# A hybrid attention and gated-recurrence encoder block: five small reorderings around its queues

## Chip, cores and metric

One core of one Trainium2 chip. The metric is the device time of one execution, in microseconds (us), as a median over several runs.

## The reference

One layer over 1024 tokens of width 1024, all in float32:

```python
u = rmsnorm(h); proj = u @ w_in                      # 1024 x 4096
qa, ka, va, hq, hff, hfb, hi, hg = split(proj, 8)    # 512 columns each
y_na = neighbourhood_attention(qa, ka, va, ...)      # 8 heads of 64
k, log_f = gate(hff or hfb, lower_bound)             # f = lb + (1-lb)*sigmoid
# S_t = diag(f_t) S_{t-1} + k_t v_t^T ; o_t = S_t^T q_t   forward and backward
y_hg = rmsnorm(o_fwd + o_bwd) * silu(hg)             # 4 heads of 128
h = h + concat(y_na, y_hg) @ w_out
u = rmsnorm(h)
h = h + square(relu(u @ w_up)) @ w_down              # hidden 4096
```

## The kernel before

Every large product is made of three float32r products (high part times high part, high times low, low times high), so each operand is split into a high part (a rounded copy) and a low part (the difference). TensorE (PE) has a list of work written out by hand, and so have VectorE (DVE), ScalarE (ACT), GpSimd (POOL) and SyncE (SP, which issues most transfers). The engines meet by counting semaphores; each executes its own list strictly in order.

**Input weights.** The 32 column tiles of w_in (128 columns each) and the 8 row tiles of w_out are loaded by SP in turn into two slots of `stage`, and POOL splits them into a ring of four slots (`w_hi`, `w_lo`): tile n is split in two instructions, `w_hi` (stage times one) and `w_lo` (stage minus w_hi). The split of tile n waits until PE has used n-3 tiles (`w_used`); SP's load of tile n waits until tile n-2 is split (`w_split`, L727). Tiles 16 to 27 hold the recurrence's gates and queries (ff, fb, hq of heads 0 to 3), 28 to 31 the output gates hg, 32 to 39 w_out. Tiles 16 to 35 are split in a loop with a register (L864 to L867, the instructions at L845 and L848), 36 to 39 at L884 to L895. Ahead of the load of tile 36 SP also waits for the first level of head 3 and then loads the attention's results back (`na_back`, 2 MB, L721), and ahead of tile 37 it waits for the outputs of head 3 and loads the residual (L726).

**The recurrence.** Head by head (h = 0 to 3), each in ten pieces. Pieces 0 to 7 each have a level: PE multiplies keys by queries for two groups of four chunks (L2073), DVE multiplies the keys (`move_keys`, L1551 and L1554) and then, for each group, the queries (L1562) and copies the level's scores under a mask (L1567, `take_level`), which lets the level after the next start. Piece 8 has the chunk updates (transposes L2092, products L2100, on DVE the chain of states L1587), piece 9 the head's outputs (L2112 to L2116). Between them PE works off the projections of the next head in steps (`take_steps`; a step is 3 matmuls of 512 columns). A projection ends in a unit of ACT or DVE that empties its bank: for hq it is ACT's copy into `h_q` (L982), which level 0 of the next head waits for, and DVE's `first_queries` (L1530) too. ACT executes the units of a piece at the piece after it (`last`); in piece 9 it squares both halves of the head's outputs (`head_squares`, L1108) ahead of that. For heads 1 and 2 the second half of hq ends in piece 9 of the head before; for head 3 it ends in piece 8.

**The output projection.** Blocks of two row tiles: block 0 needs tiles 32 and 33 split, and `mixer_hi(0)` (L1130, ACT) and `mixer_lo(0)` (L1610, DVE) of na_back. `mixer_hi(0)` stands in piece 9 of head 3, ahead of the squares.

**The MLP.** Both products are made by a scheme of seven products of half-size blocks, which needs sums of blocks of operands. Of the tokens, T1 = high - low and T3 = high's right half - T1 are formed by POOL for each of four token tiles (`token_sums`, L906 and L908) once DVE has normalised the tile t+4 (L1382); T2 is then formed by DVE (`t2_sums`, L1745). PE transposes the sets (`turn_set`, L1952); the set of T1 and T3 waits for all eight sums (`t13_sum`). ACT takes each transposed set (L1139) and DVE its low part (L1391). The up projection's product waits for the low parts of its set (L2241), POOL forms the low parts of the weights (`up_lo`, L899). At the end DVE adds the results into `acc` (L1881), in quarters: the sums number 3 fill acc_a's right half, number 4 acc_b's right half, number 5 acc_a's left half, number 6 acc_b's left half, and SP stores acc_a and acc_b by whole token tiles of 512 KB after sums 5 and 6 (L828).

Of the kernel before, what the change touches and what calls it, by code (L numbers as in the profile page):

```python
# [10 lines left out]
ALU = mybir.AluOpType  # L11
# [3 lines left out]
D = 1024  # L15
S = 1024
KT = D // P
TT = S // P
HALF = 512
# [20 lines left out]
HG_HEADS = 4  # L40
# [30 lines left out]
DOWNS = 4  # L71
# [109 lines left out]
def hybrid_block(nc, x, w_in, w_out, attn_norm_w, mlp_norm_w, q_norm_w, k_norm_w, rpb, hg_norm_w,  # L181
                 lb_fwd, lb_bwd, w_up, w_down, tables, masks, out):
    ctx = ExitStack()
    with ctx:
# [451 lines left out]
        def _(sp):  # L636
# [185 lines left out]
                load_acts(m)  # L822

            out_v = out.rearrange("b (t p) d -> (b t) p d", p=P)
            for i in range(2):
                for t in range(4):
                    sp.wait_ge(summed, 28 * (DOWNS - 1) + 4 * (5 + i) + t + 1)
                    sp.dma_start(out_v[4 * i + t], acc[i][:, t, :]).then_inc(out_store, 16)  # L828
            sp.wait_ge(h_store, 16 * TT)
            for i in range(7):  # L830
                sp.wait_ge(a_store[i], 16 * UPS)
            sp.wait_ge(out_store, 16 * TT)

            sp.wait_ge(v_stored[0], 32 * 4)
            sp.wait_ge(v_stored[1], 32 * 4)
# [3 lines left out]
        def _(pool):  # L839
# [22 lines left out]
            def split_turns(first, end):  # L862

                with pool.Fori(first, end, 1) as r:  # L864
                    for i in range(RING):
                        split(i, r * (16 * RING // STAGE) + 16 * (i // STAGE + 1) - 32,
                              r * RING + (i + 1 - RING), r * (2 * RING) + 2 * i)  # L867
# [11 lines left out]
            for n in range(RING, 4 * RING):  # L879
                if 10 <= n < 16:  # L880
                    pool.wait_ge(bias_done, bias_ops(2 * n - 19))
                split_one(n)
            split_turns(4, N_TILES // RING - 1)
            for n in range(N_TILES - 4, N_TILES):  # L884
                pool.wait_ge(w_load[n % STAGE], 16 * (n // STAGE - 1))
                if n < N_TILES - 2:
# [24 lines left out]
                up_lo(n)  # L911
            for t in range(3):
                token_sums(t)
            token_sums(3)
            up_lo(4)
            up_lo(5)
            for n in range(6, 7 * UPS):
# [8 lines left out]
        def _(act):  # L926
# [176 lines left out]
            def head_squares(h):  # L1103
                for part in range(2):
                    act.wait_ge(o_done, 2 * h + part + 1)
                    if h:
                        act.wait_ge(o_norm, 2 * h)
                    act.activation(tmp[:, part, :], bank[6 + part][:, :], ACT.Square).then_inc(o_sq, 1)  # L1108
# [162 lines left out]
            for h in range(HG_HEADS):  # L1271
                for i in range(PIECES):
                    if 1 <= i <= NHALF:
                        copy_keys(h, i - 1)
                    if i == 0:
                        for n in last:
                            unit(n)
                        last = []
                        take_diagonal(h)
                        if h:  # L1280
                            head_roots(h - 1)
                    if i == 8:
                        take_k_tok(h)
                    for n in last:
                        unit(n)
                    if i == 9:
                        if h == HG_HEADS - 1:
                            mixer_hi(0)
                        head_squares(h)
                    last = HEAD_UNITS[h][i]  # L1290

            for n in last:
                unit(n)
# [73 lines left out]
        def _(dve):  # L1367
# [386 lines left out]
            for n in range(4, 8):  # L1754
                up_sum(n)
            normalise_tokens(1, TT - 1)
            for t in range(3):
                t2_sums(t)
            take_set(8)
# [124 lines left out]
        def _(pe):  # L1884
# [285 lines left out]
            for h in range(HG_HEADS):  # L2170
                for i in range(PIECES):
                    steps = UNIT_STEPS[h][i]
                    if i < NLEV:
                        level(h, i)
                        if i == 0 and h:
                            head_means(h - 1)
                        take_steps(steps)
                    elif i == 8:
                        chunk_products(h, lambda q: take_steps(steps[len(steps) * q // 4:len(steps) * (q + 1) // 4]))
                    else:  # L2180
                        take_steps(steps)
                        head_outputs(h)
# [124 lines left out]
```

## Time and profile before

| | |
|---|---|
| median of 3 runs (lowest, highest) | 1332.29 us (1330.5, 1332.58) |
| the profiled execution | 1328.1 us |
| its span | 1326.1 us |
| PE busy in the span | 1288.4 us (97%) |
| DVE, ACT, POOL busy | 868.7 us (66%), 583.4 us (44%), 481.4 us (36%) |
| granted TensorE clock | 0.999 of full speed |
| share of the chain that ended last | PE 85%, DVE 7%, ACT 3%, issue 3%, POOL 1%, DMA 1% |

An instruction of PE is shown as busy until its last result is out, and matmuls overlap: one of 512 columns lasts 0.39 us in the rows, but starts 0.23 us after the one before. "issue" is time in which the engine waited for nothing that the profile shows. The stages of the span by the lines of PE: values and tokens first, attention's products from 103 to 304 us, the recurrence behind them, the output projection from 599 to 693 us, the up projection to 1015 us, then the down projection.

### The profile page before, as it was taken

The page shows a single profiled execution, that of the slowest core. Times are in us where ns is not written, and L with a number is a line of the kernel's source. Part 1 is how long each engine was busy: PE and PEld are TensorE (multiplying, and loading weights), DVE is VectorE, ACT ScalarE, POOL GpSimd, SP SyncE. Part 2 cuts the span into 40 slices and gives each one's busy share as a digit, 9 for nine tenths or more (in the row PEclk, how much of TensorE's full clock was granted, in tenths as well). Part 3 has the DMA queues.
Part 4 walks back from the last instruction along what each step waited for, and adds up shares of the span by engine and source line. Part 5 has one row for each costly group of instructions (what it writes and reads, how often), then busy time and mean ns, then how long its engine had stood idle before and what let it go on. Part 6 is the DMA issues. An engine that isn't in the chain of part 4 may idle for free.

```text
span 1326.1 us, 17670 instructions
## 1 busy us (share of the span) xinstructions
PE 1288.4 (97%) x6432; PEld 1077.5 (81%) x6432; DVE 868.7 (66%) x1258; ACT 583.4 (44%) x1049; POOL 481.4 (36%) x261
## 2 busy tenths in 40 slices
PE   7999899999999999899999999999999999999998
PEld 5867787998888888787887788888888788888887
DVE  3456567541878686977457655455455898888885
ACT  5436566445335353333145545445544333432341
POOL 3251121125312132212424554545443454444452
PEclk9999999999999999999999999999999999999999
DMA  8341332322111011023420654444468563443433
GB/s 256 109 129 30 77 105 83 84 73 64 35 31 33 17 32 33 20 93 144 142 94 2 207 175 135 148 155 151 135 220 320 200 239 108 139 162 112 146 99 137
DMA packets 133172, 154.91 MB, mean 117 GB/s; under 512 B 11232, under 2 KB 89312, under 8 KB 133088
## 3 DMA queue, kind: packets, MB, share of 16 engines
q1 hardware_dynamic: 128880, 147.04, 34.5%
q10 hardware_dynamic: 4208, 6.76, 1.5%
q8 instruction: 53, 0.87, 0.3%
q14 instruction: 31, 0.25, 0.1%
HBM read 109.72 MB, written 44.04 MB: 116 GB/s over the span
## 4 chain that ended last, share of the span: by engine, by line
PE 85%; DVE 7%; ACT 3%; issue 3%; POOL 1%; DMA 1%; SPq 0%; ACTq 0%; DVEq 0%
PE bank L2272 8%; PE bank L2276 8%; PE bank L2275 8%; PE bank L2241 7%; PE bank L2244 7%; PE bank L2245 7%; PE bank L1989 5%; PE bank L1993 5%; PE bank L1992 5%; PE bank L2073 4%; PE bank L2198 2%; PE bank L2202 2%; PE bank L2201 2%; PE bank L1887 1%; PE bank L1979 1%
## 5 line engine op out<-in xcount | busy, mean ns | idle before, releaser
L922 POOL TENSOR_TENSOR a_split<-a_raw,a_split 128x1024 fp32r<-128x1024 f32 x56 | 148.1, 2662 | 166.0 <-ACT a_split L1195 166.0
L2241 PE MATMUL bank<-set,w_hi 128*128 128x512 f32 x448 | 177.8, 397 | 1.0 <-issue 0.6
L2244 PE MATMUL bank<-set,w_hi 128*128 128x512 f32 x448 | 176.2, 393 | 0.0
L2245 PE MATMUL bank<-set,w_lo 128*128 128x512 f32 x448 | 176.0, 393 | 0.0
L2272 PE MATMUL bank<-w_hi,a_split 128*128 128x512 f32 x448 | 174.7, 390 | 0.2
L2275 PE MATMUL bank<-w_lo,a_split 128*128 128x512 f32 x448 | 174.3, 389 | 0.0
L2276 PE MATMUL bank<-w_hi,a_split 128*128 128x512 f32 x448 | 174.3, 389 | 0.0
L1989 PE MATMUL bank<-uT_hi,w_hi 128*128 128x512 f32 x384 | 160.8, 419 | 2.6 <-DVE h_gate L1437 2.4
L1993 PE MATMUL bank<-uT_hi,w_lo 128*128 128x512 f32 x384 | 150.6, 392 | 0.0
L1992 PE MATMUL bank<-uT_lo,w_hi 128*128 128x512 f32 x384 | 150.0, 391 | 0.0
L845 POOL TENSOR_TENSOR w_hi<-stage,one_col 128x1024 fp32r<-128x1024 f32 x20 | 39.7, 1986 | 270.9 <-PE bank L1989 223.6
L899 POOL TENSOR_TENSOR w_lo<-stage,w_hi 128x512 fp32r<-128x512 f32 x56 | 75.2, 1347 | 86.6 <-ACT w_hi L1149 86.6
L899 POOL TENSOR_TENSOR w_lo<-raw_b,w_hi 128x512 fp32r<-128x512 f32 x56 | 74.5, 1336 | 73.5 <-ACT w_hi L1149 73.5
L2241 PEld LDWEIGHTS bank<-set,w_hi 128*128 128x128 f32 x448 | 84.2, 188 | 20.9 <-issue 1.3
L2245 PEld LDWEIGHTS bank<-set,w_lo 128*128 128x128 f32 x448 | 84.1, 188 | 19.2
L2272 PEld LDWEIGHTS bank<-w_hi,a_split 128*128 128x128 f32 x448 | 84.1, 188 | 18.8 <-issue 1.7
L2244 PEld LDWEIGHTS bank<-set,w_hi 128*128 128x128 f32 x448 | 84.2, 188 | 18.2
L2276 PEld LDWEIGHTS bank<-w_hi,a_split 128*128 128x128 f32 x448 | 84.1, 188 | 17.6
L2275 PEld LDWEIGHTS bank<-w_lo,a_split 128*128 128x128 f32 x448 | 84.1, 188 | 17.5
L1837 DVE TENSOR_TENSOR w_lo<-raw,w_hi 128x1024 fp32r<-128x1024 f32 x35 | 73.4, 2103 | 26.0 <-ACT w_hi L1186 26.0
L1989 PEld LDWEIGHTS bank<-uT_hi,w_hi 128*128 128x128 f32 x384 | 72.6, 189 | 17.7 <-DVE h_gate L1437 3.2
L1186 ACT ACTIVATE w_hi<-raw 128x1024 fp32r<-128x1024 f32 x35 | 36.9, 1054 | 110.7 <-DVE raw L1835 31.6
(223 smaller groups left out, 2805.7 us busy)
## 6 DMA issues: line engine op xcount, KB each, us to landing
a_raw<-a_dram SPq DMA_DIRECT2D x56, 512.0 KB, 3.6
a_dram<-abuf SPq DMA_DIRECT2D x111, 256.0 KB, 2.1
stage<-in_w_in SPq DMA_DIRECT2D x29, 512.0 KB, 4.3
raw<-in_w_down SPq DMA_DIRECT2D x10, 1024.0 KB, 8.3
stage<-in_w_up SPq DMA_DIRECT2D x16, 512.0 KB, 5.5
raw_b<-in_w_up SPq DMA_DIRECT2D x16, 512.0 KB, 5.6
x_tok<-in_x SPq DMA_DIRECT2D x8, 512.0 KB, 10.1
v_dram<-vs ACTq DMA_DIRECT2D x16, 256.0 KB, 2.4
```

Source lines behind the costliest of these rows:

```text
L899: pool.tensor_tensor(ring_part(w_lo, n), up_operand(*UP_SEQ[n]), ring_part(w_hi, n).bitcast(F32), ALU.subtract).then_inc(x_lo, 1)
L922: pool.tensor_tensor(split_of(m, 1), a_raw[:, m % 4, :, :], split_of(m, 0).bitcast(F32), ALU.subtract).then_inc(b_lo, 1)
L1837: dve.tensor_tensor(down_slot(w_lo, m), here, down_slot(w_hi, m).bitcast(F32), ALU.subtract).then_inc(v_lo_done, 1)
L1989: first = pe.matmul(b[:, :], w[0], u[0], start=k == 0, stop=False)
L1992: pe.matmul(b[:, :], w[0], u[1], start=False, stop=False)
L1993: ins = pe.matmul(b[:, :], w[1], u[0], start=False, stop=k == KT - 1)
L2241: first = pe.matmul(dst, w[0], u[0], start=k == 0 and p in (1, 5, 6, 7), stop=False, skip_group_check=True)
L2244: pe.matmul(dst, w[0], u[1], start=False, stop=False, skip_group_check=True)
L2245: ins = pe.matmul(dst, w[1], u[0], start=False, stop=k == 3, skip_group_check=True)
L2272: first = pe.matmul(dst, a[0], w[0], start=start, stop=False, skip_group_check=True)
L2275: pe.matmul(dst, a[0], w[1], start=False, stop=False, skip_group_check=True)
L2276: ins = pe.matmul(dst, a[1], w[0], start=False, stop=q == 1 and k == 1, skip_group_check=True)
```

## The change

1. In piece 9 ACT executes the hq units of that piece ahead of the squares, not after them.
2. PE takes two steps (6 matmuls) of piece 0 of head 0 ahead of level 0, not after it.
3. POOL's splits of tiles 32 to 35 are written out, and the one of tile 33 waits until all levels of head 3 are taken (`lev_taken` at 56). Tiles 34 and 35 stand behind it.
4. T1 and T3 of the last token tile are formed by DVE behind its last normalisation, ahead of the T2 sums, and POOL waits for them in their place ahead of `up_lo(4)`.
5. The output is stored by half token tiles of 256 KB, 16 stores in place of 8, each after the sum that completes it.

```diff
-            for i in range(2):
+            for i, half, s in ((0, 1, 3), (1, 1, 4), (0, 0, 5), (1, 0, 6)):
+                cols = slice(HALF * half, HALF * half + HALF)
                 for t in range(4):
-                    sp.wait_ge(summed, 28 * (DOWNS - 1) + 4 * (5 + i) + t + 1)
-                    sp.dma_start(out_v[4 * i + t], acc[i][:, t, :]).then_inc(out_store, 16)
+                    sp.wait_ge(summed, 28 * (DOWNS - 1) + 4 * s + t + 1)
+                    sp.dma_start(out_v[4 * i + t][:, cols], acc[i][:, t, cols]).then_inc(out_store, 16)
...
-            sp.wait_ge(out_store, 16 * TT)
+            sp.wait_ge(out_store, 16 * 2 * TT)
...
-            split_turns(4, N_TILES // RING - 1)
+            split_turns(4, N_IN // RING)
+            for n in range(N_IN, N_IN + RING):
+                if n == N_IN + 1:
+                    pool.wait_ge(lev_taken, HEAD_PARTS * HG_HEADS)
+                split_one(n)
...
-            token_sums(3)
+            pool.wait_ge(t13_sum, 8)
...
                     if i == 9:
                         if h == HG_HEADS - 1:
                             mixer_hi(0)
+                        early = [n for n in HEAD_UNITS[h][i] if UNITS[n][0] == "hq"]
+                        for n in early:
+                            unit(n)
                         head_squares(h)
-                    last = HEAD_UNITS[h][i]
+                    last = [n for n in HEAD_UNITS[h][i] if i < 9 or UNITS[n][0] != "hq"]
...
             normalise_tokens(1, TT - 1)
+            dve.wait_ge(u_ready, 2 * TT)
+            dve.wait_ge(t13_sum, 6)
+            low, high = u_tok[:, 3, 0:HALF], u_tok[:, TT - 1, 0:HALF]
+            dve.tensor_tensor(low, high, low, ALU.subtract).then_inc(t13_sum, 1)
+            dve.wait_ge(t13_sum, 7)
+            dve.tensor_tensor(high, u_tok[:, TT - 1, HALF:D], high, ALU.subtract).then_inc(t13_sum, 1)
             for t in range(3):
                 t2_sums(t)
...
                     if i < NLEV:
+                        ahead = 2 if (h, i) == (0, 0) else 0
+                        take_steps(steps[:ahead])
                         level(h, i)
                         if i == 0 and h:
                             head_means(h - 1)
-                        take_steps(steps)
+                        take_steps(steps[ahead:])
```

## Rows read from the trace of the kernel before

**Rows 1.** Waits of PE over the whole span (total us, times, longest us).

```profile
PE bank L2073 <- issue: 3.2, 3, 1.2
```

**Rows 2.** Timeline, PE and ACT at the turn from head 0 to head 1.

```profile
399.14 2.02 PE L2073 MATMUL bank<-h_q,k_both 128*128 128x128 f32 x16 [1.22 <-issue]
...
398.45 0.59 ACT L982 ACTIVATE h_q<-bank 128x512 f32<-128x512 f32 x1
```

**Rows 3.** Timeline of PE, DVE and POOL at the start of head 0.

```profile
338.41 2.02 PE L2073 MATMUL bank<-h_q,k_both 128*128 128x128 f32 x16 [0.73 <-issue]
...
349.24 2.42 PE L2073 MATMUL bank<-queries,near_keys 128*128 128x128 f32 x16
...
338.35 2.36 DVE L1530 TENSOR_TENSOR queries<-forget,h_q 128x1024 f32<-128x1024 f32 x2 [5.61 <-ACT h_q L982]
...
341.76 2.84 DVE L1551 TENSOR_TENSOR near_keys<-near_keys,forget 128x512 f32<-128x512 f32 x1
344.52 3.33 DVE L1554 TENSOR_TENSOR far_keys<-near_keys,forget 128x512 f32<-128x512 f32 x1
...
348.37 0.72 DVE L1567 COPY_PREDICATED scores<-hg_mask,bank 128x512 f32<-128x512 uint8 x1
...
340.75 2.84 POOL L845 TENSOR_TENSOR w_hi<-stage,one_col 128x1024 fp32r<-128x1024 f32 x1 [9.27 <-PE bank L1989]
```

**Rows 4.** Timeline of PE, DVE and POOL in the levels of head 3.

```profile
560.67 1.13 PE L2073 MATMUL bank<-queries,near_keys 128*128 128x128 f32 x8 [0.83 <-DVE scores L1567]
563.42 1.13 PE L2073 MATMUL bank<-queries,near_keys 128*128 128x128 f32 x8 [1.62 <-DVE scores L1567]
568.37 0.50 PE L1989 MATMUL bank<-uT_hi,w_hi 128*128 128x512 f32 x1 [1.07 <-DVE h_gate L1437]
...
557.50 2.38 DVE L1562 TENSOR_TENSOR queries<-queries,decay 128x512 f32<-128x512 f32 x1
...
560.42 2.22 DVE L1562 TENSOR_TENSOR queries<-queries,decay 128x512 f32<-128x512 f32 x1
...
565.11 0.68 DVE L1562 TENSOR_TENSOR queries<-queries,decay 128x512 f32<-128x512 f32 x1
...
557.43 1.90 POOL L845 TENSOR_TENSOR w_hi<-stage,one_col 128x1024 fp32r<-128x1024 f32 x1 [13.28 <-PE bank L1989]
559.41 2.68 POOL L848 TENSOR_TENSOR w_lo<-stage,w_hi 128x1024 fp32r<-128x1024 f32 x1
```

**Rows 5.** Timeline of DVE, POOL and ACT behind the levels of heads 2 and 3.

```profile
577.99 0.73 DVE L1567 COPY_PREDICATED scores<-hg_mask,bank 128x512 f32<-128x512 uint8 x1
...
516.90 2.26 DVE L1587 SCALAR_TENSOR_TENSOR state<-state,decay,bank 128x128 f32<-128x128 f32 x6
...
517.49 1.90 POOL L845 TENSOR_TENSOR w_hi<-stage,one_col 128x1024 fp32r<-128x1024 f32 x1 [15.72 <-PE bank L1989]
...
594.35 1.99 ACT L1130 ACTIVATE acts<-na_back 128x1024 fp32r<-128x1024 f32 x2
```

**Rows 6.** Transfers of the window 490 to 620 (KB each, median us to landing).

```profile
na_back<-na_dram SPq DMA_DIRECT2D x1, 2048.0 KB, 9.6
```

**Rows 7.** Timeline of PE, DVE and POOL at the start of the MLP.

```profile
702.41 0.66 PE L1952 MATMUL bank<-tab,u_tok 128*128 128x128 f32 x4 [1.45 <-POOL u_tok L908]
...
709.36 0.47 PE L2241 MATMUL bank<-set,w_hi 128*128 128x512 f32 x1 [0.63 <-issue]
...
698.85 4.05 DVE L1745 TENSOR_TENSOR abuf<-u_tok 128x512 f32<-128x512 f32 x3
705.57 0.69 DVE L1391 TENSOR_TENSOR set<-bank,set 128x512 fp32r<-128x512 f32 x1 [2.67 <-ACT set L1139]
...
699.00 1.68 POOL L906 TENSOR_TENSOR u_tok<-u_tok 128x512 f32<-128x512 f32 x1 [3.63 <-DVE u_tok L1382]
```

**Rows 8.** Transfers of the last 9 us, and of the whole span (KB each, median us to landing).

```profile
out<-acc_b SPq DMA_DIRECT2D x4, 512.0 KB, 2.6
...
a_dram<-abuf SPq DMA_DIRECT2D x111, 256.0 KB, 2.1
```

## The prediction

> **What bounds the kernel now.** I read the page first: PE is busy for 1288.4 us of a span of 1326.1, its clock is granted in full, and the chain that ended last lies on PE for 85%. So nothing is won except where PE stands still (37.7 us in all), and nothing is lost unless PE is made to stand. The change adds and removes no matmul. So I read PE's waits and went to each that the change touches. The wait at level 0 of a head is there three times, 3.2 us in all [rows 1]. At the turn from head 0 to head 1 PE idles 1.22 us and starts level 0 as soon as ACT has copied the second half of hq; ACT starts that copy at 398.45, straight behind the square of the last outputs [rows 2]. The third wait is at head 0, 0.73 us, behind the same kind of copy [rows 3]. In head 3 the waits of 0.83, 1.62 and 1.07 us are for DVE, and DVE there has no idle time: two of its multiplications last 2.38 and 2.22 us where the same one lasts 0.68 [rows 4]. At the MLP's start PE waits 1.45 us for POOL's last sum, and soon after 0.63 us for a set [rows 7]. At the end the last store takes 2.6 us from issue to landing [rows 8].
>
> **How DVE and POOL get in each other's way.** This rule is read from the rows and priced below. The multiplication that starts at 557.50 ends at 559.88; POOL's w_hi ends at 559.33. The one that starts at 560.42 ends at 562.64; POOL's w_lo ends at 562.09 [rows 4]. In both cases DVE ends 0.55 us after POOL, about its own working time. So an instruction of DVE with two operands in SBUF stands still until POOL's running instruction is through. It costs 1.70 + 1.54 = 3.24 us in this split. The instructions with one operand in PSUM don't stand: the six of the state chain that start at 516.90 take 2.26 us with POOL's split beginning at 517.49 under them [rows 5], hence 0.38 each.
>
> **The change, part by part.**
>
> *hq ahead of the squares.* The copy (0.59 us) moves to a place where ACT waits for the outputs anyway. Level 0 of heads 1 and 2 can then follow the last output without a gap: 1.22 us for the row shown, and (3.2 - 0.73) / 2 = 1.24 for each of the two [rows 1 to 3]. DVE's first_queries waits for the last output as well, so it moves forward by about 1.1 us with PE, and what follows keeps its order. Behind the copy in ACT's queue stand only the two squares, whose average PE takes after level 0 (2.02 us), so they have cover. Value: 2.4 us; ends 2.2 and 2.5. The third wait belongs to part 2, since head 3's hq ends a piece earlier.
>
> *Two steps ahead of level 0 in head 0.* They are 6 matmuls at 0.23 us = 1.4 us, and cover the 0.73 us wait. But what is late next is DVE. It works without a gap from 338.35 on, and hands over the first level at 348.37 + 0.72 = 349.09; PE starts the level after the next at 349.24 [rows 3]. So PE has 0.15 us to win there, not 0.73. The moved steps also release POOL's split earlier: the first of them ends at about 338.0, so the split would start near 338.1 and not at 340.75, under first_queries in place of under the key multiplications. Now its two instructions stretch the multiplications of 341.76 and 344.52; moved, the same two stand in the same unbroken line of DVE work, so its end stays where it is. Level 1 may wait some 1.4 us for the second half of the queries, out of the 1.4 us that PE has gained on it. Value: 0; ends -0.3 and 0.7.
>
> *The split of tile 33 behind the last level.* It takes the block of 3.24 us out of a DVE chain that PE waits on. Without it the waits of 0.83 and 1.62 us go, and of the third (1.07) 0.8: PE is earlier by 2.45, DVE by 3.24, so 0.3 us stays [rows 4]. Value 3.2; ends 2.4 (the third wait stays) and 3.5 (all three go). What is queued behind the wait: on POOL the splits of 33, 34 and 35; on SP the load of tile 35, behind it na_back, behind that tile 36. The last level is taken at G = 577.99 + 0.73 = 578.72 [rows 5]; PE's level 7 sets it, so it keeps its distance to PE. Split 33 is done at G + 1.90 + 0.1 + 2.68 = G + 4.7, split 34 at G + 9.4 or sooner. Split 34 (now near 578) then lies under the state chain, which doesn't stand for it. PE needs 32 and 33 only past its outputs at 599 = G + 20: covered. na_back is issued some tenths behind the load ahead of it, I take G + 5.1, and takes 9.6 us [rows 6], so it lands at G + 14.7; ACT's mixer_hi takes it at 594.35 = G + 15.6 [rows 5]. Cover 0.9 us. If that cover is gone, ACT's squares of the last head come late behind it, and PE after them.
>
> *T1 and T3 on DVE.* POOL starts them at 699.00 and PE goes at 702.41 [rows 7]. DVE is free at 698.9; two dependent instructions of 0.68 with 0.1 between are done at 700.3, before PE is ready for them (702.41 - 1.45 = 700.96). The wait of 1.45 us goes. What is late next: three T2 sums stand behind them on DVE. Now they last 4.05 us, against POOL's last two sums; then they meet POOL's up_lo(4) and (5), released at the same moment, so I give them the same 4.05: they end at 700.3 + 4.05 = 704.35, and the low part of the first set starts there and not at 705.57, 1.2 us earlier. The product at 709.36 waits for the fourth such part, so PE is 1.2 us earlier, not 1.45 [rows 7]. Value 1.2; ends 0.6 (DVE loses both races against POOL) and 1.45.
>
> *Half stores.* The last sum is where it was. The last store has 256 KB in place of 512: the nearest row of that size, and of the same 2 KB rows, lands in 2.1 us against 2.6 [rows 8]. The eight stores of the right halves are issued earlier, under matmuls. All loads stand ahead of them on SP. Value 0.5; ends 0.2 and 0.7.
>
> The Trainium skill (DMA: Bandwidth & Descriptors, "Bandwidth") tells to batch transfers up to 1 MiB or more, which speaks against this part; its fixed share of about 2.0 us and 436 GB/s would make, as an estimate, 3.2 and 2.6 us of the two sizes, so a gain of 0.6, on a level that the trace shows lower by 0.5.
>
> **Sum.** 2.4 + 0 + 3.2 + 1.2 + 0.5 = 7.3 us. The profiled execution of 1328.1 us becomes 1320.8. The median of the runs, 1332.29, lies 4.2 us above that execution, with all three runs above it; I take the gain off the median: 1325.0 us. A measurement can tell about 0.2% (2.7 us) from no change.
>
> **Rivals.**
>
> *A. Slower: na_back becomes the wait.* Place: ACT's mixer_hi(0) in piece 9 of head 3. For: the cover is 0.9 us, and tile 35, na_back and tile 36 now leave within a few us. Each us of landing past G + 15.6, and what room there is behind it (I take 0.5 us), is paid by PE. It loses the other parts' gain at a landing of 9.6 + 1.4 + 7.3 = 18.3 us, and shows as slower from 21 us; at 22 us the time is 1336. Against: the landing was measured with the load of tile 35 just ahead of it, as it will be. 4%.
>
> *B. The gate gives back what it won.* Either na_back lands 2 to 4 us late, or the state chain does stand for split 33 and 34 (up to 1.90 + 2.68 us). Then 3.2 is returned: 1328.2; with part of the T1/T3 gain gone too, 1329 to 1330. Against: the chain's 2.26 us over a split [rows 5]. 20%, 8% of it within 0.2% of before.
>
> *C. The T1/T3 sums only trade one wait for another.* PE then waits at the set of 709.36 instead: 0.6 of the part stays, or nothing. 1325.6 to 1326.2. 12%.
>
> *D. The stores queue on one another.* If a 256 KB store held its queue for its whole 2.1 us, four at PE's pace of 1.36 us per sum (6 matmuls) would end 4 x 2.1 - 3 x 1.36 = 4.3 us after the first, 1.7 later than the 2.6 of now: 1327.2. That is how the skill's batching rule would show here. Against: 512 KB stores at the same pace land in 2.6 us each. 3%.
>
> *E. The steps ahead pay in full,* because POOL and DVE meet elsewhere: 1324.3, or 1323 with all other upper ends. 6%.
>
> The forecast itself has the other 55%.
>
> **Chances and range.** Faster by over 0.2%: forecast 55, C 12, D 3, E 6 and B's other 12 make 88; I hold back 4 for runs that scatter by 2 us and 1 for what I haven't seen: 83%. Within: B's 8 and the 4, 12%. Slower: A's 4 and the 1, 5%. Below, 1332.3 - 8.8 (all upper ends: 2.5 + 0.7 + 3.5 + 1.45 + 0.7) = 1323.4, less 1.6 for scatter (half the spread of the three runs is 1.0) is 1321.8. Above, B's 1328.2 and 1.1 for scatter: 1329.3.
>
> **What would show it.** Right: PE's waits at level 0 gone; DVE's L1562 in head 3 at 0.68 throughout; splits of 33 and 34 back to back past the last level; the 1.45 us before L1952 gone and the one at L2241 grown to some 0.9; the last landing at 2.1. PE starting level 2 of head 0 at about 349.2 as before shows part 2 at nothing. Wrong: an idle ACT ahead of L1130 with na_back as its releaser, L1587 longer than 0.38, a new PE wait at L2198, or a new wait anywhere in the MLP's first 60 us, where DVE, ACT and POOL run close to each other.

## The result and the profile after

| | before | after |
|---|---|---|
| median of the runs (lowest, highest) | 1332.19 us (1330.5, 1332.58) | 1322.27 us (1318.37, 1322.97) |
| the profiled execution | 1328.1 us | 1322.97 us |
| its span | 1326.1 us | 1321.0 us |
| PE busy | 1288.4 us (97%) | 1289.5 us (98%) |
| DVE, ACT, POOL busy | 868.7, 583.4, 481.4 us | 868.1, 583.6, 478.3 us |
| granted TensorE clock | 0.999 | 0.996 |

Four runs of each kernel; the ratio is 0.9932 with an interval of 0.9916 to 0.9949, so a gain of 6.8 to 11.2 us. The medians lie 9.9 us apart. I had forecast 1325.0, and the measured time lies in the range. The two profiled executions differ by 5.1 us only; why three numbers for one gain (9.9, 5.1, and 8.0 below) fit together is part of what follows.

The waits of PE after the change (total us, times, longest us), those in the stages that the change touches:

```profile
PE bank L2003 <- DVE h_gate L1445: 2.1, 3, 1.0
PE bank L2257 <- issue: 1.1, 1, 1.1
PE bank L2087 <- DVE queries L1538: 0.8, 1, 0.8
```

L2087 is the line of the levels (L2073 before), L2257 the up projection's product (L2241). The three waits of 3.2 us at level 0 [rows 1] are no longer in the list, nor is a wait for `u_tok`. The two largest waits for `scores` [rows 4] are gone too. New is 0.8 us for `queries`, at level 1 of head 0.

The start of head 0, and the turn from head 0 to head 1, in the timeline of after:

```profile
347.27 1.57 PE L2087 MATMUL bank<-queries,near_keys 128*128 128x128 f32 x8 [0.82 <-DVE queries L1538]
...
341.27 5.95 DVE L1538 TENSOR_TENSOR queries<-forget,h_q 128x1024 f32<-128x1024 f32 x2 [5.61 <-ACT h_q L987]
...
340.91 1.89 POOL L846 TENSOR_TENSOR w_hi<-stage,one_col 128x1024 fp32r<-128x1024 f32 x1 [6.51 <-PE bank L2003]
342.88 3.24 POOL L849 TENSOR_TENSOR w_lo<-stage,w_hi 128x1024 fp32r<-128x1024 f32 x1
...
400.39 1.95 PE L2087 MATMUL bank<-h_q,k_both 128*128 128x128 f32 x16
...
395.68 0.60 ACT L987 ACTIVATE h_q<-bank 128x512 f32<-128x512 f32 x1 [6.22 <-PE bank L2007]
398.13 0.60 ACT L1113 ACTIVATE tmp<-bank 128x512 f32<-128x512 f32 x1 [1.86 <-PE bank L2130]
```

At the turn the copy of hq is through by 396.28 and level 0 starts at 400.39 with no wait ahead of it, where PE had stood 1.22 us [rows 2]. At head 0 POOL's split now lies under `first_queries` (5.95 us in place of 2.36) and no longer under the two multiplications of the keys [rows 3].

Head 3, from its fourth level to the output projection:

```profile
557.52 0.69 DVE L1570 TENSOR_TENSOR queries<-queries,decay 128x512 f32<-128x512 f32 x1
...
581.03 2.26 DVE L1595 SCALAR_TENSOR_TENSOR state<-state,decay,bank 128x128 f32<-128x128 f32 x6
...
565.18 0.50 PE L2003 MATMUL bank<-uT_hi,w_hi 128*128 128x512 f32 x1 [0.76 <-DVE h_gate L1445]
...
575.59 1.90 POOL L874 TENSOR_TENSOR w_hi<-stage,one_col 128x1024 fp32r<-128x1024 f32 x1 [31.40 <-DVE scores L1575]
577.56 2.38 POOL L877 TENSOR_TENSOR w_lo<-stage,w_hi 128x1024 fp32r<-128x1024 f32 x1
579.90 1.89 POOL L874 TENSOR_TENSOR w_hi<-stage,one_col 128x1024 fp32r<-128x1024 f32 x1
...
580.48 0.38 SPq L721 DMA_DIRECT2D na_back<-na_dram  x1
...
591.15 1.99 ACT L1135 ACTIVATE acts<-na_back 128x1024 fp32r<-128x1024 f32 x2
```

DVE's multiplications of the queries last 0.69 where two of them lasted 2.38 and 2.22 [rows 4]. POOL's splits of tiles 33 and 34 stand behind the last level, back to back, and the chain of states has its old 2.26 us over the second of them. na_back is issued at 580.48 and lands 8.9 us later, at 589.4; ACT takes it at 591.15 without waiting.

The start of the MLP:

```profile
695.78 0.69 DVE L1768 TENSOR_TENSOR u_tok<-u_tok 128x512 f32<-128x512 f32 x1
696.51 0.69 DVE L1770 TENSOR_TENSOR u_tok<-u_tok 128x512 f32<-128x512 f32 x1
697.12 4.08 DVE L1753 TENSOR_TENSOR abuf<-u_tok 128x512 f32<-128x512 f32 x3
...
697.28 1.67 POOL L904 TENSOR_TENSOR w_lo<-stage,w_hi 128x512 fp32r<-128x512 f32 x1 [5.08 <-DVE u_tok L1770]
698.91 1.74 POOL L904 TENSOR_TENSOR w_lo<-raw_b,w_hi 128x512 fp32r<-128x512 f32 x1
...
704.89 0.47 PE L2257 MATMUL bank<-set,w_hi 128*128 128x512 f32 x1 [1.05 <-issue]
```

The two sums on DVE take 0.69 us each, and the three T2 sums behind them 4.08 us, against POOL's two `up_lo`. PE's wait of 1.45 us is gone and the one at the fourth product is 1.05 us in place of 0.63 [rows 7].

The last transfers (KB each, median us to landing):

```profile
out<-acc_b SPq DMA_DIRECT2D x4, 256.0 KB, 2.0
```

### The profile page after: what moved, and what is told of

It reads as the page before. It is cut to its first block, busy times and chain, and to the rows that moved or that the text cites. A ratio compares the mean times of both kernels' runs of the same rounds, so it can differ in the third digit from the quotient of the medians.

```text
span 1321.0 us, 17673 instructions
## 1 busy us (share of the span) xinstructions
PE 1289.5 (98%) x6432; PEld 1079.9 (82%) x6432; DVE 868.1 (66%) x1260; ACT 583.6 (44%) x1049; POOL 478.3 (36%) x259
## 4 chain that ended last, share of the span: by engine, by line
PE 84%; DVE 8%; ACT 3%; issue 2%; DMA 1%; POOL 1%; SPq 0%; ACTq 0%; DVEq 0%
PE bank L2288 8%; PE bank L2292 8%; PE bank L2291 8%; PE bank L2257 7%; PE bank L2260 7%; PE bank L2261 7%; PE bank L2003 5%; PE bank L2007 5%; PE bank L2006 5%; PE bank L2087 3%; PE bank L2214 2%; PE bank L2218 2%; PE bank L2217 2%; PE bank L1901 1%; PE bank L1990 1%
## 5 line engine op out<-in xcount | busy, mean ns | idle before, releaser
L2257 PE MATMUL bank<-set,w_hi 128*128 128x512 f32 x448 | 177.8, 397 | 1.4 <-issue 1.1
L874 POOL TENSOR_TENSOR w_hi<-stage,one_col 128x1024 fp32r<-128x1024 f32 x16 | 30.4, 1902 | 228.1 <-DVE bias L1489 95.9
L846 POOL TENSOR_TENSOR w_hi<-stage,one_col 128x1024 fp32r<-128x1024 f32 x16 | 32.3, 2019 | 205.0 <-PE bank L2003 174.5
L2257 PEld LDWEIGHTS bank<-set,w_hi 128*128 128x128 f32 x448 | 84.2, 188 | 21.3 <-issue 1.7
```

Source lines behind the costliest of these rows:

```text
L2257: first = pe.matmul(dst, w[0], u[0], start=k == 0 and p in (1, 5, 6, 7), stop=False, skip_group_check=True)
```

## A ledger of PE's time

Runs of one kernel differ by 2 us and more, as much as most of the parts are worth. So every trace was cut at the same places of PE's list, and the stretches compared: from the end of the last first-head projection (the steps taken ahead left out) to level 0 of head 1, from there to those of heads 2 and 3, from level 0 of head 3 to the first product of the up projection, from there to a product some 64 us on, past the MLP's start, then to the start of DVE's last sum, and from that to the span's end. Where the code of a stretch is the same, it repeats within 0.1 us from trace to trace, but for three things that are spoken of below: a wait for `s` of 0.2 to 0.8 us and the last T1 sum, both in the MLP's start, and a wait of 1.2 us early in the down projection, in the column "rest". In us:

| | head 0 | head 1 | head 2 | head 3 to first up product | MLP's start | rest | tail | sum |
|---|---|---|---|---|---|---|---|---|
| before | 61.62 | 62.03 | 66.18 | 165.96 | 64.98 | 563.79 | 4.01 | 988.57 |
| after | 59.95 | 60.83 | 66.10 | 162.81 | 63.67 | 563.79 | 3.38 | 980.53 |
| hq alone | 60.27 | 60.86 | 66.11 | 165.97 | 65.50 | 563.78 | 4.01 | 986.50 |
| steps alone | 61.31 | 61.99 | 66.20 | 166.00 | 64.94 | 563.80 | 4.00 | 988.24 |
| gate alone | 61.63 | 62.02 | 66.21 | 162.83 | 66.11 | 563.77 | 4.00 | 986.57 |
| T1/T3 alone | 61.69 | 62.01 | 66.20 | 166.00 | 63.92 | 563.74 | 4.00 | 987.56 |
| stores alone | 61.67 | 62.01 | 66.18 | 165.95 | 64.98 | 564.58 | 3.37 | 988.74 |

After is 8.04 us shorter than before. The parts alone give: hq 1.35 + 1.17 + 0.07 = 2.6; steps 0.31; gate 3.13; T1/T3 1.06; stores 0.64. That is 7.7, and the parts add up: head 0's 1.67 is 1.35 + 0.31, head 3's 3.15 is the gate's. The excess of 0.5 in hq alone, and of 0.8 in the stores alone, stand in stretches which these parts don't touch and are spoken of below.

## The experiments

The kernels ran on three chips, each time beside the kernel before on the same chip: its medians there were 1330.3 (13 runs), 1331.7 (one run) and 1329.85 us (9 runs).

**Each part by itself.** First the gate: before, with the splits of tiles 32 to 35 written out and the wait in them.

```diff
-            split_turns(4, N_TILES // RING - 1)
+            split_turns(4, N_IN // RING)
+            for n in range(N_IN, N_IN + RING):
+                if n == N_IN + 1:
+                    pool.wait_ge(lev_taken, HEAD_PARTS * HG_HEADS)
+                split_one(n)
```

> The kernel before with the gated split alone. Lock theory: 3.2 us less, 1329.0, with head 3's first two scores waits gone, the h_gate wait of 1.07 at 0.8, and ACT's mixer_hi not waiting for na_back (issue to landing 9 to 10 us, on hand about 1 us early). Rival (na_back takes the place): an idle ACT ahead of mixer_hi and 0 to 1 us gained.

Measured: 1327.37 us (6 runs), ratio 0.9969 (0.9957 to 0.9982), so 2.4 to 5.7 us less than before by the interval; the ledger gives 3.13 for head 3. The MLP's start took 1.13 us more than in before, though nothing of it was edited (0.4 of it is the wait for `s`, 0.6 us here):

```profile
697.35 1.89 DVE L1749 TENSOR_TENSOR abuf<-u_tok 128x512 f32<-128x512 f32 x3
...
697.51 2.86 POOL L910 TENSOR_TENSOR u_tok<-u_tok 128x512 f32<-128x512 f32 x1 [3.63 <-DVE u_tok L1386]
...
701.76 0.66 PE L1956 MATMUL bank<-tab,u_tok 128*128 128x128 f32 x4 [2.29 <-POOL u_tok L912]
```

Here DVE's T2 sums last 1.89 us and POOL's T1 2.86, where in before it is 4.05 and 1.68 [rows 7]. The same two neighbours start the same 0.16 us apart, DVE first. In before POOL stands for DVE's first sum only and gets in ahead of the second; here it stands until all three are through. PE's wait is 2.29 in place of 1.45. So the stage has two outcomes, 0.8 us apart, and which one comes is not set by the code of the stage. In the traces of the kernels that keep this stage as it was, one showed this outcome and four the other. T1 and T3 on DVE take the race away from PE's path.

Then the hq units ahead of the squares, the two steps ahead of level 0, T1 and T3 on DVE, and the half stores, each alone on top of before, one run each.

```diff
+                        early = [n for n in HEAD_UNITS[h][i] if UNITS[n][0] == "hq"]
+                        for n in early:
+                            unit(n)
                         head_squares(h)
-                    last = HEAD_UNITS[h][i]
+                    last = [n for n in HEAD_UNITS[h][i] if i < 9 or UNITS[n][0] != "hq"]
```

> The kernel before with ACT's hq copy ahead of the squares alone. PE's waits of 1.22 us ahead of level 0 of heads 1 and 2 go, 0.73 in head 0 stays. Theory: 2.4 us less between level 0 of head 0 and level 0 of head 3. Rival (the changed profile's 0.24 us that turned up between level 0 and level 1 of heads 1 and 2 come from the other parts): 2.2 or less here.

Measured: 1329.07 us, with 1331.7 for before beside it. The waits of heads 1 and 2 at level 0 are gone, and that of head 0 (0.73 us) stays. Worth 2.6 us by the ledger. In this trace PE waits 0.8 us for `s` in the MLP's start, where before has 0.2.

```diff
+                        ahead = 2 if (h, i) == (0, 0) else 0
+                        take_steps(steps[:ahead])
                         level(h, i)
...
-                        take_steps(steps)
+                        take_steps(steps[ahead:])
```

> The kernel before with the two steps ahead of level 0 alone. Theory (DVE is the bound of head 0's first levels): the wait of 0.73 us ahead of level 0 goes, a wait of 0.7 to 1.4 us for DVE's queries comes at level 1, and from level 3 on PE is only 0 to 0.4 us earlier than before, counted from the last projection ahead of the head. Rival (full pay): 0.7 us earlier throughout.

Measured: 1327.71 us, a single run, 4.0 us below the single run of before beside it; the ledger has 0.31 us, all of it in head 0, and nothing elsewhere. The run lists a clock of 0.999 and the one beside it 0.996, which is two falls of the clock less, some 3.4 us (the last section has their price). That one number of a run and one stretch of a trace differ so much is the reason why the small parts were read from the ledger.

```profile
344.16 1.57 PE L2073 MATMUL bank<-queries,near_keys 128*128 128x128 f32 x8 [0.81 <-DVE queries L1530]
...
338.16 5.95 DVE L1530 TENSOR_TENSOR queries<-forget,h_q 128x1024 f32<-128x1024 f32 x2 [5.61 <-ACT h_q L982]
...
347.87 0.73 DVE L1567 COPY_PREDICATED scores<-hg_mask,bank 128x512 f32<-128x512 uint8 x1
```

From the start of `first_queries` to the first scores DVE takes 347.87 - 338.16 = 9.71 us, and took 348.37 - 338.35 = 10.02 in before [rows 3]. The moved split blocks DVE for 5.95 - 2.36 = 3.59 us; where it was, it blocked it for 2.84 + 3.33 less the 1.13 us that each of the two multiplications takes here unblocked, 3.91 us. The difference, 0.32, is the part's gain.

```diff
-            token_sums(3)
+            pool.wait_ge(t13_sum, 8)
...
+            dve.wait_ge(u_ready, 2 * TT)
+            dve.wait_ge(t13_sum, 6)
+            low, high = u_tok[:, 3, 0:HALF], u_tok[:, TT - 1, 0:HALF]
+            dve.tensor_tensor(low, high, low, ALU.subtract).then_inc(t13_sum, 1)
+            dve.wait_ge(t13_sum, 7)
+            dve.tensor_tensor(high, u_tok[:, TT - 1, HALF:D], high, ALU.subtract).then_inc(t13_sum, 1)
```

> The kernel before with T1 and T3 of the last token on DVE alone. The 1.45 us wait at L1952's set goes, the wait at L2241 (0.63) is 0.8 to 1.1: 1.2 to 1.3 us less from the first up product to the wait at 758. If the race theory is right, no execution can show the 2.29 us wait any more, since POOL has no last T1 to form.

Measured: 1326.46 us, one run; before's median beside it 1329.85. The wait for `u_tok` is gone, the one at the fourth product is 1.05 us, and that for `s` 0.55 in place of 0.2, which is what makes 1.06 in this ledger and 1.31 in after's.

```diff
-            for i in range(2):
+            for i, half, s in ((0, 1, 3), (1, 1, 4), (0, 0, 5), (1, 0, 6)):
+                cols = slice(HALF * half, HALF * half + HALF)
                 for t in range(4):
-                    sp.wait_ge(summed, 28 * (DOWNS - 1) + 4 * (5 + i) + t + 1)
-                    sp.dma_start(out_v[4 * i + t], acc[i][:, t, :]).then_inc(out_store, 16)
+                    sp.wait_ge(summed, 28 * (DOWNS - 1) + 4 * s + t + 1)
+                    sp.dma_start(out_v[4 * i + t][:, cols], acc[i][:, t, cols]).then_inc(out_store, 16)
```

> The kernel before with half stores alone. From the last sum of DVE to the end 3.4 us in place of 4.0, the last landing 2.0 to 2.1 in place of 2.6; nothing else moves.

Measured: 1328.8 us, one run. The tail from the last sum is 3.37 us in place of 4.01, and the last stores land in 2.0 us. But the trace has a wait of PE of 1.2 us in the down projection, at 1040 us:

```profile
1035.77 1.06 ACT L1196 ACTIVATE a_split<-a_raw 128x1024 fp32r<-128x1024 f32 x1 [0.36 <-DMA a_raw<-a_dram]
1036.58 1.22 DVE L1830 TENSOR_TENSOR raw<-raw 128x1024 f32<-128x1024 f32 x1
1036.91 3.13 POOL L923 TENSOR_TENSOR a_split<-a_raw,a_split 128x1024 fp32r<-128x1024 f32 x1 [3.85 <-ACT a_split L1196]
1040.14 0.47 PE L2273 MATMUL bank<-w_hi,a_split 128*128 128x512 f32 x1 [1.22 <-issue]
```

The row names no releaser, but PE's product waits in the kernel for POOL's low part (`b_lo`), and that is through at 1040.04. It is late because a load of `a_raw` landed late: 15.6 us from issue, where the same load takes 13.7 to 14.9 in the twelve traces without a wait of this length. So ACT waits 0.36 us for it, POOL starts behind DVE's sum of 1036.58 and stands for it, 3.13 us in place of 2.49. In before POOL starts first, at 1035.98, and DVE's sum of 1036.13 stands, 3.42 us in place of 1.22.

The output's stores begin far behind this place, so the part doesn't cause it. The same wait stood in one other trace (the one with only POOL held back in the MLP, below), behind the same load, and in none of the other twelve, after's two among them. Why the load is late in these two is open.

**All but the gate.** After, without its wait.

```diff
-                if n == N_IN + 1:
-                    pool.wait_ge(lev_taken, HEAD_PARTS * HG_HEADS)
```

> The changed kernel without the wait of the split of tile 33 (four parts left). Lock theory (a DVE instruction with two SBUF operands stands until POOL's running instruction ends): two of the L1570 multiplications in head 3 are at 2.2 to 2.4 us again, PE's waits of 0.8 and 1.6 us for DVE's scores are back, and the stretch from level 0 to the outputs of head 3 is 3.2 us longer than in the changed kernel; time about 1325.5. Rival (the gain of the gate is given back behind the levels, at na_back or the state chain): less than 1 us longer.

Measured: 1324.99 us (7 runs), ratio 0.9964 (0.9951 to 0.9976). In the ledger head 3 lasts 167.06 us, not before's 165.96 but 1.1 more, and 4.25 more than after's. The timeline of DVE, POOL and PE:

```profile
554.52 1.75 DVE L1568 TENSOR_TENSOR queries<-queries,decay 128x512 f32<-128x512 f32 x1
...
556.82 1.76 DVE L1544 TENSOR_TENSOR decay<-decay 128x64 f32<-128x64 f32 x1
...
553.29 2.44 POOL L874 TENSOR_TENSOR w_hi<-stage,one_col 128x1024 fp32r<-128x1024 f32 x1 [13.34 <-PE bank L2001]
555.81 2.69 POOL L877 TENSOR_TENSOR w_lo<-stage,w_hi 128x1024 fp32r<-128x1024 f32 x1
...
563.56 0.50 PE L2001 MATMUL bank<-uT_hi,w_hi 128*128 128x512 f32 x1 [2.59 <-DVE h_gate L1443]
```

The split blocks DVE here for (1.75 - 0.69) + (1.76 - 0.22) = 2.6 us (0.22 us is the same instruction's time in after), and PE waits 2.59 us in one piece. Behind that wait the clock falls, as the windows show (PE busy, PEld, DVE, ACT, POOL; PEclk; DMA share; GB/s):

```profile
560.00:564.00 4.00, 1.41 (x7) 0.85 (x6) 3.90 (x8) 1.76 (x3) 0.00 (x0) 1.00 0.97 335
564.00:568.00 4.00, 4.00 (x20) 3.88 (x19) 3.47 (x7) 1.98 (x3) 0.00 (x0) 0.57 0.79 312
```

A mean of 0.57 in 4 us is 3.4 us at half, the level of 1.2 GHz; half of 3.4 us of work is lost, 1.7 us. Without it the missing gate costs 4.25 - 1.7 = 2.6 us in this kernel, just what the split blocks. On top of before the gate is worth 3.1, since there the split's two instructions blocked DVE for 3.24. What I had expected was 3.2 us, with two multiplications at 2.2 to 2.4 us and PE's waits of 0.8 and 1.6 us back; the cause came as put, but the split meets other instructions of DVE here, and the fall of the clock was not in the sum. The trace also shows the reverse: POOL's w_hi starts together with DVE's multiplication of 553.29 and takes 2.44 us where it takes 1.90 elsewhere.

**A longer gate, and na_back's cover.** In these two kernels tile 32's split is held back as well (the wait at N_IN, not N_IN + 1). In the second, SP also loads na_back ahead of tile 34 and not of tile 36:

```diff
-                if n == N_IN + 1:
+                if n == N_IN:
                     pool.wait_ge(lev_taken, HEAD_PARTS * HG_HEADS)
...
-                if n == N_IN + RING:
+                if n == N_IN + 2:
                     sp.wait_ge(*level_done(HG_HEADS - 1, 0, 1))
```

> The changed kernel with the wait one tile earlier, ahead of the split of tile 32. The block of 3.6 us that this split makes on DVE goes (L1559 and L1562 in head 3 at 0.68 throughout), and with it PE's waits of 1.00 and 0.76 us for h_gate: 1.7 us gained in the levels. But na_back now stands behind two gated splits: issued at G + 9.2, landed at G + 18.1, where ACT wants it at G + 15.6 (G: last level taken). If the rival of the prediction on na_back is the right price list (each us past 15.6 paid, less some 0.5 of room), 1.3 to 2 us go back: time within 0.7 us of the changed kernel, with ACT idle 2.5 us ahead of mixer_hi and a new PE wait at the first output product. If na_back has more room than I think: 1.7 us less than the changed kernel.

Measured: 1324.03 us (5 runs), ratio 0.9952 (0.9937 to 0.9967). The levels of head 3 are 2.44 us shorter than in after, since DVE is now free of POOL through all of them, and the stretch as a whole is 2.12 us longer (164.93 against 162.81). What it turned into:

```profile
588.67 2.01 ACT L1135 ACTIVATE acts<-na_back 128x1024 fp32r<-128x1024 f32 x2 [3.51 <-DMA na_back<-na_dram]
...
589.76 2.36 DVE L1618 TENSOR_TENSOR acts<-na_back,acts 128x1024 fp32r<-128x1024 f32 x2 [3.05 <-ACT acts L1135]
...
592.23 0.77 PE L2214 MATMUL bank<-w_hi,acts 128*128 128x512 f32 x1 [3.20 <-issue]
```

na_back was issued at 577.99 and landed in 10.6 us, and ACT waited 3.51 us for it. DVE's low parts of the same operand (`mixer_lo`, which PE's first output product waits for) came behind and were through at 592.12, and PE stood 3.20 us until 592.23, after which the clock fell:

```profile
591.00:595.00 4.00, 2.77 (x7) 2.25 (x8) 1.82 (x2) 2.52 (x5) 1.86 (x1) 0.58 1.03 400
```

That is rival A of the prediction, in the place where it was put, one gate further on. But PE was reached through `mixer_lo`, and not through ACT's squares as the rival has it: the squares were done at 591.64, and their product (L2137) stands behind the first output products.

> As the run before, and SP loads na_back ahead of tile 34 and not of 36, so that it leaves in head 3's levels. ACT's wait for na_back goes; 1.7 us less than the changed kernel if nothing else is late. Rival: the splits of 32, 33 and 34 now run back to back for 13 us past the last level, and the multiplication L1436 (two SBUF operands) between the two state chains, at G + 9.7, is blocked by up to 1.9 us; then the outputs' wait for the states shows 0.5 to 1.5 us on PE.

Measured: 1320.07 us (4 runs), ratio 0.992 (0.9903 to 0.9937). The load is issued at 536.04, with nothing ahead of it, and ACT takes the data at 587.58 without a wait:

```profile
587.58 1.99 ACT L1135 ACTIVATE acts<-na_back 128x1024 fp32r<-128x1024 f32 x2
```

The stretch is 160.42 us, 2.4 less than after's and 4.5 less than with the late load. So all of that loss came from na_back, with the fall of the clock that the wait for it brought. The wait of 0.76 us at 565.18 is gone too.

**The wait left at the MLP's start.** Two kernels on top of after. The first holds POOL's `up_lo(4)` until DVE's T2 sums are through; the second also changes DVE's order, so that the low part of the second set comes ahead of the first T4 sums.

```diff
-            pool.wait_ge(t13_sum, 8)
+            pool.wait_ge(t2_sum, 3)
```

> The changed kernel, with POOL's low part number 4 of the up weights waiting for three T2 sums in place of the eight T1 and T3 sums. Contest theory (the 4.08 us of the three T2 sums are POOL's two instructions in their way): they take 1.9 us, the set's first low part starts when ACT's copy is there, 0.4 us earlier, and PE's wait of 1.05 at L2257 falls to 0.65. Rival (ACT or PE is the bound of that set): the wait stays at 1.05.

```diff
-            for t in range(4):
-                take_set(10 + t)
-                t4_sums(t)
+            take_set(10)
+            take_set(11)
+            t4_sums(0)
+            for t in range(1, 3):
+                take_set(11 + t)
+                t4_sums(t)
+            t4_sums(3)
```

> As the run before, and DVE forms the low part of the set's fourth tile ahead of the first T4 sum. The wait at L2257 falls by another 0.6 us, to 0 or 0.1; if what follows on DVE (T4 sums, later low parts) has no room, up to 0.6 us comes back as a wait at a later transposition or product before 760 us.

Measured: 1323.38 and 1319.9 us, one run each. The first:

```profile
696.95 1.89 DVE L1753 TENSOR_TENSOR abuf<-u_tok 128x512 f32<-128x512 f32 x3
700.55 0.69 DVE L1399 TENSOR_TENSOR set<-bank,set 128x512 fp32r<-128x512 f32 x1 [1.72 <-ACT set L1144]
...
704.50 0.47 PE L2257 MATMUL bank<-set,w_hi 128*128 128x512 f32 x1 [0.85 <-issue]
```

The T2 sums fell from 4.08 to 1.89, and PE's wait by 0.2 only (0.4 expected), for now DVE waits 1.72 us for ACT's copy of the set. With the order changed it is 0.25 us (0 to 0.1 expected):

```profile
701.85 0.47 PE L2261 MATMUL bank<-set,w_hi 128*128 128x512 f32 x1 [0.25 <-issue]
```

By the ledger the second kernel has 0.76 us over after (62.91 against 63.67 at the MLP's start), the first 0.22.

**After once more, and all of it together.** The last two timed kernels are after unchanged, and after with both tiles gated, na_back early, POOL held and DVE's order changed (the edits shown above).

> The changed kernel itself, beside the kernel before on one chip. By the parts read from the traces (0.3 + 2.5 + 3.2 + 1.3 + 0.6) 8.0 us less than before; if the kernel before loses the race for its last T1 in some executions (2.29 in place of 1.45 us, as in the run with the gate alone) 8 to 9 us. Rival (the 9.9 us of the first comparison hold): 9.5 or more.

> The changed kernel with both gates (splits of tiles 32 and 33 behind the last level), na_back loaded ahead of tile 34, POOL's up_lo(4) held for the T2 sums and the set's fourth low part ahead of the T4 sums. If the gains add up: 2.3 + 0.8 = 3 us less than the changed kernel, about 11 us less than before. Rival (the late wait at L2257 near 750 us grows, as it did to 0.6 with the gates): 2.5 less than the changed kernel.

Measured: after 1321.33 us (5 runs, 1318.15 to 1322.47), ratio 0.9934 (0.9917 to 0.9951); the new one 1318.25 us (5 runs, 1316.69 to 1320.14), ratio 0.9918 (0.9902 to 0.9933). After's second median is 8.5 us below before's: nearer to the 8.0 of the parts than to the rival's 9.5, though the interval (6.5 to 11.0 us) excludes neither. The medians of after and of the new kernel on this chip are 3.1 us apart, their ledgers 2.98. The two intervals overlap, so the runs alone don't separate them; the ledger does, with 160.44 against 162.85 for head 3's stretch and 63.29 against 63.92 for the MLP's start. It is the fastest kernel of this study, 11.6 us below before's median beside it.

## Why the prediction held, and where it didn't

| part | predicted | ends | measured |
|---|---|---|---|
| hq ahead of the squares | 2.4 | 2.2 to 2.5 | 2.6 |
| two steps ahead | 0 | -0.3 to 0.7 | 0.3 |
| gate | 3.2 | 2.4 to 3.5 | 3.1 |
| T1/T3 | 1.2 | 0.6 to 1.45 | 1.3 (1.06 alone) |
| half stores | 0.5 | 0.2 to 0.7 | 0.6 |
| sum | 7.3 | | 8.0 |

*hq.* The mechanism is as put: the copy moved into ACT's idle time, and level 0 follows the outputs. The term was 0.1 to 0.2 too small. A wait costs PE more than the idle time that its row names: past 565.18 in after the next matmul starts 0.33 us later and not 0.23, and the idle is counted from the modelled end of the one before, 0.16 behind its pitch (0.39 - 0.23).

*The steps.* Here a step of the argument failed, if by little. I held that the two blocks "stand in the same unbroken line of DVE work, so its end stays where it is". They do stand there, but they block for 3.59 us and not for 3.91. The order of late things was right: PE's level 1 waits, 0.8 us where I had some 1.4, and DVE's chain, not hq's copy, sets level 2.

*The gate.* The reading that a DVE instruction with two operands in SBUF stands still until POOL's is through held in head 3: behind the gate there is no split beside the levels, and no multiplication over 0.69. The one split that is left beside them is tile 32's, from 539.50 on, and the two multiplications of the keys that it meets take 2.17 and 2.87 us and end 0.55 us behind POOL, as at [rows 4]. What the reading lacks is its other side: POOL stands as well where DVE's instruction began first (2.44 us at the split without the gate, 2.86 at the last T1). The chain of states took 2.26 us over split 34, as at [rows 5]. The Trainium skill (SBUF — State Buffer, "Who interferes with whom") states both halves, that a DVE instruction with two SBUF inputs contends with a POOL instruction that reads SBUF, and that one with at most one such input, outside two-port modes, doesn't. The traces agree, with 1.75 against 0.69 us and with 2.26 against 2.26. I had 0.3 us left of the third wait, and 0.76 was left; yet the gain is as forecast, since the two waits that went paid more than their rows, for the reason just given: level 7 starts 44.54 us behind level 0 and started 47.71 behind it. The timing of what was queued behind the gate came out close: with the last level taken at G = 575.51, split 33 is done at G + 4.4 (I had 4.7), na_back is issued at G + 5.0 (5.1), lands at G + 13.9 (14.7), and is taken at G + 15.6 (15.6). The cover was 1.8 us, not 0.9, because this load took 8.9 us and not 9.6; before's profiled execution has the longest landing of the eleven traces in which it is issued ahead of tile 36 and behind no second gated split, and the other ten have 8.6 to 9.1. Rival A didn't come; that it was a real one the longer gate shows. There the load is issued behind two gated splits, at G + 9.3 and not G + 5.0, and lands in 10.6 us and not 8.9, while ACT asks for it 0.8 us later behind G: 1.8 + 0.8 - 4.3 - 1.7 = -3.4, the wait of 3.5 us. Rival B's other half, the chain of states standing for the splits, didn't come either.

*T1 and T3.* One wait of 1.45 us went and another grew from 0.63 to 1.05 (I had 0.9); the T2 sums have 4.08 us (I had 4.05). What was not in the forecast is the second outcome of the race between DVE and POOL at this place. It makes before slower by 0.8 us in the executions in which POOL loses, and so the part worth more in the runs than in before's profiled execution. Rival C, in which no more than half would stay, is out: 1.3 of 1.45 stayed.

*Stores.* 2.6 to 2.0 us from issue to landing, as the row of the same size had it (2.1). Rival D is out: four stores behind one another land in 2.0 each. The gain of 0.6 is the one of the estimate from the Trainium skill's figures (about 2.0 us and 436 GB/s; they stand in DMA: Bandwidth & Descriptors, "Anatomy of one DMA — SWDGE (gpsimd) path", for transfers that GpSimd issues, and here SP does), while both landings lie 0.6 below its level. The Trainium skill's advice to batch to 1 MiB (DMA: Bandwidth & Descriptors, "Bandwidth") would have cost this 0.6 us at a transfer that nothing follows.

*From the sum to the time.* The ledger's 8.04 us is what the five parts do, and the interval of the runs, 6.8 to 11.2 us, holds it. The profiled execution of after shows 5.1 of it, since its last first-head projection ends at 340.44 where before's ended at 337.52: 2.9 us were lost ahead of everything that the change touches, where after has two falls of the clock more (below), and 8.0 - 2.9 = 5.1. The medians show 9.9 and, in the second comparison, 8.5. What they have over the ledger, 0.5 to 1.9 us, is no more than what single runs of one kernel scatter (after's four lie 4.6 us apart); the race at T1 may hold a part of it. I didn't separate the two. So 1325.0 was 2.7 us too high: 0.7 of it stands in the terms, and 2.0 in what the ledger doesn't hold. The measured 1322.27 lies 0.5 us inside the lower end of my range, and one of its four runs below that end. What the trace confirms is the sum of the parts; that the median stayed inside is in part luck.

## What to carry to other kernels

Where two engines block each other for whole instructions, the place of a long instruction in the slower engine's queue is a free variable: put it where the other has idle time, or where its instructions read PSUM, and follow what is queued behind it, here a 2 MB load whose cover was 1.8 us. Before the queue is held back longer, move the load, not the gate: the same gate lost 2.1 us and won 2.4. And for parts of less than 2 us read stretches of the trace between fixed points of the bounding engine's list; runs and whole spans carry the clock's scatter with them.

## What the runs showed of the hardware beside this

The granted clock falls to its half, 1.2 GHz, for 3.4 us at a time behind single waits of an otherwise busy PE, and each fall costs 1.7 us of PE's work. In after, behind the wait of 4.60 us that ends at 146.41, there are two falls on end:

```profile
144.00:148.00 4.00, 1.59 (x7) 1.62 (x8) 0.00 (x0) 0.00 (x0) 0.00 (x0) 0.68 0.64 138
148.00:152.00 4.00, 4.00 (x14) 3.32 (x13) 2.35 (x5) 0.49 (x1) 0.00 (x0) 0.50 0.43 119
152.00:156.00 4.00, 4.00 (x22) 3.64 (x22) 1.70 (x6) 3.13 (x9) 0.00 (x0) 0.96 0.10 28
...
232.00:236.00 4.00, 2.58 (x14) 2.57 (x15) 2.48 (x10) 2.31 (x8) 0.00 (x0) 0.78 0.25 67
236.00:240.00 4.00, 4.00 (x29) 4.00 (x29) 3.93 (x9) 1.83 (x6) 3.12 (x2) 0.80 0.48 126
```

The shares below 1.00 are 4 x (0.32 + 0.50 + 0.04) = 3.4 us of lost clock in the first three windows, and 4 x (0.22 + 0.20) = 1.7 us in the last two, behind a wait of 1.8 us. In before the first place lost 4 x (0.25 + 0.18) = 1.7 us, and the second nothing, though it has the same wait:

```profile
144.00:148.00 4.00, 1.74 (x7) 1.77 (x8) 0.00 (x0) 0.08 (x1) 0.00 (x0) 0.75 0.59 137
148.00:152.00 4.00, 4.00 (x20) 3.41 (x20) 3.12 (x9) 1.55 (x5) 0.00 (x0) 0.82 0.45 120
```

The fall at the 1.8 us wait stood in six of the fourteen traces. The one at the first place stood in all, single in nine (behind waits of 4.3 to 4.5 us) and double in five (4.5 to 5.1). The waits of 2.59 and 3.20 us above had one each. Behind the wait of 1.62 us in head 3, which five of the kernels have, there was one in a single trace, the one with T1 and T3 alone, and there it cost nothing: its level took 2.05 us in place of 1.13,

```profile
562.96 2.05 PE L2079 MATMUL bank<-queries,near_keys 128*128 128x128 f32 x8 [1.62 <-DVE scores L1567]
```

but the wait of 1.07 us for `h_gate` that follows it in before [rows 4] is missing, and the stretch is the same 166.00. So a fall is worth up to 1.7 us, less what it lies in idle time or fills of a later wait. Their number sets the clock that a run lists (0.999 with one, 0.996 with three), and they are a part of the scatter of the runs: of the thirteen runs of before on one chip the three at 0.999 have a median of 1329.0 us, the six at 0.996 one of 1331.3. They are not all of it, for on another chip six runs of before at 0.997 lie 3.4 us apart. The falls are the strongest reason to go next at the waits of the attention stage, which this change leaves alone.
